# The Sigmoid of the first gate moves behind the copies that start the branch phase

## What is computed

```python
y_a = hs.astype(x.dtype) * jax.nn.gelu(lru_gate)
...
merged = jax.nn.sigmoid(gate_a) * (y_a @ lw['w_br_lru']) + jax.nn.sigmoid(gate_b) * (y_b @ lw['w_br_ssd'])
x = x + merged @ lw['w_out']
```

## Time and profile before

| | us |
|---|---|
| median of three runs | 1106.71 |
| lowest and highest | 1106.45, 1107.41 |
| the profiled execution | 1105.57 |
| its span, first to last instruction | 1103.5 |
| busy: TensorE, VectorE, ScalarE | 961.2, 590.8, 411.2 |

### The profile page before, as it was taken

One profiled execution on the slowest core, in us unless ns is written; L12 is line 12 of the kernel. 1 busy time (PEld: TensorE's weight loads), 2 busy tenths in 40 slices (PEclk: granted clock), 3 DMA queues, 4 the chain that ended last, 5 costly groups with the idle time before them and its releaser, 6 DMA issues.

```text
span 1103.5 us, 16870 instructions
## 1 busy us (share of the span) xinstructions
PE 961.2 (87%) x5421; PEld 711.1 (64%) x5421; DVE 590.8 (54%) x1062; ACT 411.2 (37%) x685; POOL 168.7 (15%) x206
## 2 busy tenths in 40 slices
PE   5497887988889888898877999986999999999895
PEld 3386766867668776687765998775444344444474
DVE  2675875758757587575875553123334233333443
ACT  3454563645536355363655331161111111111322
POOL 0043241232412414124140000000000000000000
PEclk9898998989989899898996999986999999999998
DMA  7171351814518144171543750770699999999101
GB/s 183 39 180 44 101 156 38 214 43 113 144 38 214 43 128 128 48 204 43 147 125 97 203 163 18 263 301 1 246 384 381 390 387 388 383 388 374 52 1 43
DMA packets 208584, 188.48 MB, mean 171 GB/s; under 512 B 7985, under 2 KB 166377, under 8 KB 208553
## 3 DMA queue, kind: packets, MB, share of 16 engines
q1 hardware_dynamic: 207336, 187.12, 53.0%
q10 hardware_dynamic: 1216, 0.96, 0.3%
HBM read 176.85 MB, written 11.21 MB: 170 GB/s over the span
## 4 chain that ended last, share of the span: by engine, by line
PE 68%; DVE 14%; ACT 9%; issue 6%; DMA 1%; DVEq 1%; ACTq 0%; SPq 0%
PE bank L1634 10%; PE bank L1337 6%; PE bank L1338 6%; PE bank L1339 6%; PE bank L1604 5%; PE bank L1662 5%; PE bank L1497 4%; PE bank L1611 4%; PE bank L1412 3%; PE bank L1684 3%; PE bank L1517 3%; PE bank L1501 2%; PE bank L1321 2%; DVE wlo L927 2%; DVE ii L1058 2%
## 5 line engine op out<-in xcount | busy, mean ns | idle before, releaser
L1337 PE MATMUL bank<-h_hi,whi 128*128 128x288 f32 x640 | 208.3, 326 | 29.1 <-DVE wlo L927 29.1
L1338 PE MATMUL bank<-h_lo,whi 128*128 128x288 f32 x640 | 200.2, 313 | 0.0
L1339 PE MATMUL bank<-h_hi,wlo 128*128 128x288 f32 x640 | 199.3, 311 | 0.0
L1337 PEld LDWEIGHTS bank<-h_hi,whi 128*128 128x128 f32 x640 | 131.8, 206 | 46.6 <-DVE wlo L927 33.1
L1338 PEld LDWEIGHTS bank<-h_lo,whi 128*128 128x128 f32 x640 | 131.8, 206 | 0.4
L1339 PEld LDWEIGHTS bank<-h_hi,wlo 128*128 128x128 f32 x640 | 131.5, 205 | 0.0
L1252 DVE TENSOR_TENSOR xT<-xT,bank 128x288 f32<-128x288 f32 x128 | 49.5, 449 | 150.8 <-PE bank L1611 150.8
L678 ACT ACTIVATE whi<-wb 128x1024 fp32r<-128x1024 f32 x82 | 86.7, 1059 | 99.9 <-PE bank L1339 95.7
L927 DVE TENSOR_TENSOR wlo<-wb,whi 128x1024 fp32r<-128x1024 f32 x82 | 103.5, 1263 | 20.2 <-ACT whi L678 12.3
L1604 PE MATMUL bank<-pick,htok 96*128 96x256 f32 x240 | 61.2, 398 | 4.0 <-DVE AB L1237 4.0
L858 ACT ACTIVATE Gs<-bank 128x512 f32<-128x512 f32 x16 | 9.6, 597 | 142.8 <-PE bank L1634 142.8
(11 more groups left out here) (341 smaller groups left out, 1643.2 us busy)
## 6 DMA issues: line engine op xcount, KB each, us to landing
wb<-in_w SPq DMA_DIRECT2D x80, 1024.0 KB, 8.5
wb<-in_w_in SPq DMA_DIRECT2D x80, 512.0 KB, 4.0
wb3a<-in_w SPq DMA_DIRECT2D x16, 1024.0 KB, 8.4
arena<-in_state_ssd SPq DMA_DIRECT2D x16, 512.0 KB, 5.6
out_new_ssd_s<-arena SPq DMA_DIRECT2D x16, 512.0 KB, 5.9
wb<-in_w_br_ssd SPq DMA_DIRECT2D x16, 512.0 KB, 3.9
wb<-in_w_br_lru SPq DMA_DIRECT2D x8, 512.0 KB, 3.8
wb<-in_w_out SPq DMA_DIRECT2D x8, 512.0 KB, 5.0
```

What stands on the lines that cost most here:

```text
L1337: mm(bP[i % 2][:, 0:T], hi, h_hi[:, k, :], start=(k == 0), stop=False)
L1338: mm(bP[i % 2][:, 0:T], hi, h_lo[:, k, :], start=False, stop=False)
L1339: ins = mm(bP[i % 2][:, 0:T], lo, h_hi[:, k, :], start=False, stop=(k == KC - 1))
```

## The change

In ScalarE's program behind the loop over groups, the sigmoid of `ga` is moved. Before, it stands ahead of the wait for the last `lru_tail` and the six copies to `br_hi`; after, it stands behind the copies, directly ahead of the sigmoid of `gb`.

```diff
@@ -785,13 +785,12 @@
             ch.leave(G)
 
 
-            act_f(ga[:], ga[:], ACT.Sigmoid).then_inc(gates_ready, 1)
-
             act.wait_ge(lru_tail.sem, lru_tail.at(G - 1, 1))
             for t in range(6):
                 src = ya[:, 4 * t:4 * t + 4, :] if t < 2 else yb[:, 4 * t - 8:4 * t - 4, :]
                 act_f(br_hi[:, 4 * t:4 * t + 4, :], src, ACT.Copy).then_inc(br_large.sem, 1)
             act.sem_inc(b_large.sem, 6 + 2)
+            act_f(ga[:], ga[:], ACT.Sigmoid).then_inc(gates_ready, 1)
             act_f(gb[:], gb[:], ACT.Sigmoid).then_inc(gates_ready, 1)
 
             def branch_large(i, s, slot):
```

## The result

The kernel after takes 1109.34 us, median of 20 runs, against 1106.59 for the kernel before in 20 runs taken with it. The ratio is 1.0039, with a 95% interval of 1.0026 to 1.0052: it is slower by 4.3 us, 2.9 to 5.8. The median understates this, because the times after fall into two heaps, eleven runs from 1107.8 to 1109.4 and nine from 1111.5 to 1115.0; the means are 1110.7 and 1106.4. The profiled execution is of the upper heap: it took 1113.34 us. Over the 20 runs TensorE's mean granted clock is 0.916 to 0.922 in the lower heap and 0.910 to 0.917 in the upper.

The account below looks back on a forecast made before the run. TensorE was busy 87% of the span, but at the seam before the branch phase ScalarE's order set its start. Stall 3.17 plus clock 1.5 gave 4.7 us on 1106.71: 1111.4 us, range 1109.3 to 1113.3.

Parts of the forecast that it names:

- The path: Behind the group loop, ScalarE's order sets when TensorE goes on; load and first sigmoid lay under ScalarE's wait for `lru_tail`.
- The gain: At the `br_hi` copies: without the sigmoid in front, the first copy starts 0.26 us earlier.
- The loss: Behind the copies: load and sigmoids make the first `whi` copy and TensorE's third branch step 3.17 us later.
- The drain: Rival: the load behind the copies first empties ScalarE, costing one more load's length, 1.28 us; 1112.7 us, chance 0.05.
- Another load: Rival: copies after gelu need their own table load, on the path ahead of `br_hi`; 1112.7 us, chance 0.02.
- The clock: After TensorE's 3.7 us gap before the third branch step, the clock runs low for 3.4 us, losing 1.5 us.
- The rival in which it stays up: Stall at the third step without the clock falling, as after the 2.17 us wait; 1109.9 us, chance 0.15.
- The sum: Third step's stall of 3.17 us plus 1.5 us of low clock, 4.7 us, added to median 1106.71: 1111.4 us.
- The other side: Rival: no loss, if the first `whi` copy were not awaited; 1106.4 us, at best 1104.9, chance 0.04.

Follow-up runs that it names:

- the first experiment: Kernel after plus a one-column Sigmoid ahead of the wait for the last `lru_tail`, so the table load lies under it; ratio 1.0033 to before.

## Why the prediction was right, and where it was off

**The path.** The step that carried the case was to see that the load and the sigmoid lay under ScalarE's wait, and that behind the copies there was no such cover. The trace after shows it as described: the load directly behind the copies, both sigmoids, then `whi`, the wait of line 1497 (now 1496) for `wlo` grown to 3.54 us (3.7 forecast).

**The gain.** Forecast 0.26 us; measured 0.35. The first copy starts 0.03 us behind the end of the `ya` product, not 0.12 as the row of line 781 had it. ScalarE had waited idle there as well (2.38 us), and why the two differ is not shown.

**The loss.** Forecast 3.17 us at the first `whi` copy; measured 11.82 - 8.72 = 3.10 us, each counted from the end of the `ya` product (607.96 - 599.24 = 8.72 before). The third step starts 14.17 us behind that end in place of 11.08, 3.09 later. The two experiments that take the load and the sigmoid away give 1.41 and 2.00 us, and their sum less the gain of 0.35 is 3.06.

**The drain.** The rival worked out beside the Trainium skill, "ScalarE: Activation LUTs", section "What ACT_TABLE_LOAD costs", which puts the switch at 2.66 us with a drain, did not come about, and here the load did follow copies with no wait in the program between them. The last copy ends at 602.24 + 4.31 = 606.55, the load runs from 606.57 for 1.28 us, the sigmoid starts at 607.86. The load is as long as the Trainium skill says, its drain does not show; the measurement decides. One reading of the prediction was wrong here: it said that no load in its rows has more than 1.31 us between its neighbours, but from the end of gelu (596.12) to the sigmoid (597.59) it is 1.47 us, 0.16 of them idle ahead of the load. That is still far from 2.66.

**Another load.** No load stands ahead of the copies: behind gelu, at 596.48, ScalarE's next row is the first copy at 600.12.

**The clock.** Forecast 1.5 us from the gap of 3.23 us as the nearest; measured 4.60 - 3.09 = 1.51 us in the timeline, and 1.50 us by filling the gap. It fell in all three executions seen. The rival in which it stays up was given 0.15 on the strength of the row after 2.17 us, and in the first experiment the clock fell behind a gap of 2.11 us all the same. The three rows that the prediction reads look like an order by length, and the traces as a whole do not bear that out (the rows are in the last section). The choice had better grounds than these rows: from 120 to 540 us in the kernel before, eight waits took from 3.18 to 3.28 us, and behind each of them the clock fell to 0.50 within a microsecond.

**The sum against the times.** Forecast 4.7 us at the seam; measured 4.60 there, and 4.3 us by the ratio. The median of 1109.34 lies 2.1 us under the forecast of 1111.4, 0.04 us above the lower end of the range. That it lies inside at all is luck: the median stands at the top of the lower heap, which alone runs from 1107.8 to 1109.4. The term at fault is the comparison of the sum with a median: it took the rest of the kernel as one number, where the routing stretch alone took 69.2 to 72.1 us in three executions of the same program. A median of two heaps jumps to whichever is the larger; the mean of the 20 runs, 1110.7, is 0.7 us off. The range's 0.6 us for the spread of the runs, taken from three runs of before, was too small for that.

**The other side.** Not slower would have needed 3.2 us of room at the third step. The experiment with both gates behind the `whi` copies shows that ScalarE has this room, but two instructions further on.

## What to carry to other kernels

A short engine's instruction is free only where the engine waits, so an edit that moves one is priced by the wait that it leaves and the slack that it enters, not by the engine's busy share: here 37% busy, and 3.1 us lost in full. Move such work to the next place where the same engine waits for the bound one, and move a table load by a one-column instruction ahead of a wait. A gap opened on TensorE can cost a second time through its clock, half as much again here, and the whole time of a few runs does not resolve such terms, where a stretch between two fixed instructions does.

## What the hardware showed that was not expected

The length of a single wait does not tell whether the clock falls behind it. With the load under the wait, 2.11 us of waiting was followed by 0.50, 1.4 us after the work had gone on. The kernel before kept 1.00 behind 2.17 us at line 1377 in all eight groups. In the kernel after the same wait, 2.17 us at line 1376, was followed by 0.50 in the first three groups and by 1.00 in the other five. And a wait of 3.08 us early in the kernel before left it at 1.00. The row and the stretch behind it, first after, then before:

```profile
84.09 0.48 PE L1376 MATMUL bank<-arena,cst 32*128 32x128 f32 x2 [2.17 <-ACT ex L761]
```

```profile
85.20:87.60 2.40, 2.40 (x12) 2.40 (x11) 1.19 (x4) 1.78 (x5) 0.47 (x2) 0.50 0.01 3
```

```profile
34.81 0.40 PE L1337 MATMUL bank<-h_hi,whi 128*128 128x288 f32 x1 [3.08 <-DVE wlo L927]
```

```profile
34.80:38.20 3.40, 3.39 (x25) 3.39 (x26) 2.46 (x5) 0.66 (x2) 0.00 (x0) 1.00 0.63 168
```

What decides between these cases is not shown. And executions of one program differ by 2.8 us in a stretch of some 70 us, with the same waits at the seam, while the clock's low stretches lie differently there.
